# Sliding-window attention in a four-mixer decoder trunk: mask, scale and row maximum in one operation, keys ahead of the first queries left out, three reorderings

## The chip, the cores and the metric

The kernel runs on one NeuronCore of a Trainium2 chip, all four layers in one launch. The metric is the device time in microseconds, the median of several runs. A run is compared with runs of the kernel before on the same chip.

## The reference, cut to what matters

The input is a residual stream of 512 tokens by 1024 features, batch 1. Four layers follow each other; layer i adds mixer i (RG-LRU, Mamba-2 SSD, sliding-window attention, HGRN2) and then a gated feed-forward block with a short convolution. All is float32. The change is in the third mixer:

```python
q = _partial_rope(_rmsnorm(q, q_norm), cos, sin)       # 16 heads of 64
k = _partial_rope(_rmsnorm(k, k_norm), cos, sin)       # 4 heads, each shared by 4 query heads
...
scores = jnp.einsum('bnqhgd,bnkhd->bnhgqk', qb, kw) * (hd ** -0.5)
...
mask = (diff >= 0) & (diff < WINDOW) & (kpos[:, None, :] >= 0)
scores = jnp.where(mask[None, :, None, None], scores, -jnp.inf)
...
m = jnp.maximum(jnp.max(scores, axis=-1, keepdims=True), sink)
p = jnp.exp(scores - m)
denom = jnp.sum(p, axis=-1, keepdims=True) + jnp.exp(sink - m)
o = jnp.einsum('bnhgqk,bnkhd->bnqhgd', p / denom, vw).reshape(bsz, s, nq)
return o.astype(h.dtype) @ w_out
```

Queries come in four blocks of 128; a block sees its own 128 keys and the 128 before them, within a window of 128. The first block has no keys before it. The sink is one number per head, which enters the maximum and the denominator only.

## The kernel before, in words

Features lie on the partitions and the 512 tokens along the free dimension. Each weight matrix comes in panels of 128 x 1024 (8 tiles of 128 x 128) through a ring of four slots. SyncE loads panel n once GpSimd has split panel n-4. ScalarE rounds it to a big part (`round_until`, L242 to L252), GpSimd subtracts that from the panel in four pieces of 256 columns and gets the bfloat16 rest (`weights_gpsimd`, L260 to L268), and TensorE multiplies both parts: eight products of the big part and eight of the rest for a tile of 512 tokens (L295 and L305 for the projections in, L337 and L341 for those out). ScalarE rounds a panel only when TensorE has used the one four places before it.

The third mixer has 12 projected tiles of 128 rows: two of keys, eight of queries, two of values. Query tile t holds two heads. The attention is cut into 16 units: unit un treats query tile t = un // 2 (so two heads, `a` = 0 and 1) and the blocks 2m and 2m+1 of queries with m = un % 2. It has four rows of work, one for each head and block, each 128 queries by 256 keys. For the first block of even units the 256 columns are blocks 0 and 1 of the keys, and the mask takes the second 128 out.

The order of everything is written out by hand in `swa_events` (L2091 to L2128), one list that every engine walks through, taking its own events. Slot 9 is v = 0. In slot v TensorE has scores(v), products pv(v-3), a step of the out projection (`early`, for one finished y tile; SWA_FILL says how many in which slot), and transposes turn(v-2). The last slots, v = 16 to 18, have no scores and two steps each. The steps of one unit:

- TensorE, scores (L2207): four products with 64 rows into PSUM banks 5 and 6. It waits until the DVE has masked the unit before (`swa_masked`), because the banks are reused.
- DVE, `score` in `swa_vector` (L2370 to L2389): four `scalar_tensor_tensor` (L2381), PSUM times a factor per query (`b.fq`, the query's normalisation) plus mask into SBUF; then the reciprocal of the sums of unit un-1 (L2364); then, after a wait for the sink column of un, one `tensor_reduce` (L2388) over all four rows of 257 columns for the negated maximum.
- ScalarE (L2302): four exponentials of 257 columns with the sum as an accumulated result. They wait for the reduction.
- GpSimd (`swa_gpsimd`, L2404 on): `sunk` (L2417) copies the sinks into column 256 of the four rows of a score buffer; there are three buffers, so it waits for the transposes of unit un-3. `weighted` (L2425) multiplies the four rows by the reciprocals. In its queue, among the panels: sinks 0 and 1 after panel 11; weighting 0 after panel 13; after panel 14 sink 2, weighting 1, sink 3, weighting 2; after panel 15 sink 4, weighting 3, sink 5, weighting 4, and so on to weighting 15.
- TensorE, transposes (L2224): eight of 128 x 128 into banks 7 and 4, each pair after its row is weighted and after the copies of the unit before. ScalarE copies them to SBUF (L2310, two of 512 columns, `copied`, which stands behind the exponentials of unit un+1 in its queue).
- TensorE, products with the values (L2242): eight of 128 columns; then, after each odd unit, ScalarE and the DVE split the finished y tile (L2316, L2395).

After unit 15 TensorE has the first seven steps of output tile 2 and then the rest of the out projection (`out_tensor`), which needs no attention unit but the last y tile.

Of the kernel before, what the change touches and what calls it, by code (L numbers as in the profile page):

```python
# [28 lines left out]
P = 128  # L29
# [59 lines left out]
PARAMS = {}  # L89
# [1991 lines left out]
SWA_V = 10  # L2081
SWA_FIRST = 9
# [8 lines left out]
def swa_events():  # L2091

    ev, fill = [], 0
    for slot in range(SWA_FIRST + 19):
# [18 lines left out]
        if 3 <= v:  # L2113
            ev.append(("pv", v - 3, 0))
        if v >= 0:
            for _ in range(SWA_FILL[v]):
                ev.append(("early", fill // 2, fill % 2))
                fill += 1
# [27 lines left out]
def swa_tensor(pe, k):  # L2146
# [48 lines left out]
    def score(un, _):  # L2195
        t, m = un // 2, un % 2
        pe.wait_ge(k.s("swa_rotated"), 3 * rope_index(2 + t) + 3)
        if un:
            pe.wait_ge(k.s("swa_masked"), 4 * un)
        else:  # L2200
            pe.wait_ge(k.s("swa_rotated"), 3 * rope_index(1) + 3)
        for blk in range(2):
            for a in range(2):
                rows = slice(64 * a, 64 * a + 64)
                n = 2 * m + blk
                key = max(n - 1, 0) * P
                mm = pe.matmul(k.ps[:, 5 + a, blk * 256:(blk + 1) * 256], b.q[rows, t, n * P:(n + 1) * P],  # L2207
                               b.kt[rows, t // 4, key:key + 256], start=True, stop=True)
        mm.then_inc(k.s("swa_scored"), 1)

    def turn(un, _):
# [7 lines left out]
        for a in range(2):  # L2219
            for blk in range(2):  # L2220
                pe.wait_ge(k.s("swa_weighted"), 4 * un + 2 * a + blk + 1)
                for kh in range(2):
# [4 lines left out]
    def pv(un, _):  # L2227
# [7 lines left out]
        for blk in range(2):  # L2235
            n = 2 * m + blk
            for kh in range(2):
                chunk = max(n - 1, 0) + kh
                at = (2 * blk + kh) * P
                for a in range(2):  # L2240
# [3 lines left out]
                                   start=kh == 0, stop=kh == 1)  # L2244
# [14 lines left out]
def swa_scalar(act, k):  # L2259
# [36 lines left out]
    def score(un, _):  # L2296
        m, s = un % 2, b.scores[un % 3]
        act.wait_ge(k.s("swa_max"), un + 1)
        for a in range(2):
            for blk in range(2):  # L2300
                row, n = s[:, a, blk, 0:257], 2 * a + blk
                act.activation(row, row, ACT.Exp, bias=b.neg[:, m, n:n + 1], accum_out=b.sum[:, m, n:n + 1]  # L2302
                               ).then_inc(k.s("swa_exp"), 1)

    def copied(un, _):
        if un >= 2:
            act.wait_ge(k.s("swa_pv"), un - 1)
        for a in range(2):
            act.wait_ge(k.s(f"swa_turned{a}"), un + 1)
            act.activation(b.pt[:, un % 2, a, :], k.ps[:, (7, 4)[a], :], ACT.Copy).then_inc(k.s(f"swa_pt{a}"), 1)  # L2310
# [14 lines left out]
def swa_vector(dve, k):  # L2325
# [44 lines left out]
    def score(un, _):  # L2370
# [17 lines left out]
        dve.tensor_reduce(b.neg[:, m].rearrange("p (a b) -> p a b", a=2), s[:, :, :, 0:257], AX.X, ALU.max,  # L2388
                          negate=True).then_inc(k.s("swa_max"), 1)  # L2389
# [13 lines left out]

def swa_gpsimd(pool, k, panel):  # L2404
    b = SwaBuffers(k)

    def sunk(un):
        t, s = un // 2, b.scores[un % 3]
        at = PARAMS["swa_sinks"][0] + 8 * (t // 4) + t % 4
# [294 lines left out]
```

## Time and profile before

| | |
|---|---|
| median of 3 runs | 1797.73 us |
| lowest and highest | 1797.21 and 1797.99 us |
| the profiled execution, its own time | 1797.72 us |
| its span in the profile | 1795.5 us |
| TensorE busy | 1754.2 us, 98% |
| DVE, ScalarE, GpSimd busy | 65%, 63%, 68% |
| share of TensorE in the chain that ended last | 75% |

The page of a profile gives the busy time of each engine, the span in 40 slices, the chain of work that ended last and the costliest groups of instructions. PE is TensorE, DVE VectorE, ACT ScalarE, POOL GpSimd. Times inside the profile count from the start of the span. Matmuls are pipelined and their ends are modelled, so a matmul's duration is longer than its share of TensorE's time; the distance from one start to the next tells more. The same holds on the other engines: an instruction's record can overlap the next one's. The attention units lie between about 976 and 1050 us, in slices 22 and 23 of 40.

### The profile page before, as it was taken

Reading aid. Unit: us, or ns where it says so; the run is one execution under the profiler, and the core shown is the slowest. Engines: PE = TensorE matmul, PEld = TensorE weight load, DVE = VectorE, ACT = ScalarE, POOL = GpSimd, SP = SyncE. Lnnn points to the kernel's source line nnn. Section 1 sums busy time; section 2 is a strip of 40 time slices with the busy share of each in tenths; the row PEclk is TensorE's granted clock in tenths of the full one; section 3 lists DMA queues with packets and bytes.
Section 4 is the critical chain, followed back from the end, with each engine's and each line's share of the span. In section 5 each row is a group of like instructions: output and inputs, shape, how many; then the busy total and the mean of one; then the engine's idle time right before and its main releaser. Section 6 shows DMA issues by size and latency. Waiting matters only on the chain.

```text
span 1795.5 us, 25084 instructions
## 1 busy us (share of the span) xinstructions
PE 1754.2 (98%) x8752; PEld 1086.2 (60%) x8752; DVE 1166.7 (65%) x1884; ACT 1130.1 (63%) x1582; POOL 1220.6 (68%) x1776
## 2 busy tenths in 40 slices
PE   7989999999999999999999999999999999999999
PEld 4546666655565556666666666666667766566665
DVE  6886777138988855777237857774267777577720
ACT  8887666456887667666464877665444444866641
POOL 7847777876545467777875658777864444577785
PEclk9999999999999999999999999999999999999999
DMA  7333444444222235444442024444432232244443
GB/s 267 105 95 129 151 143 144 160 149 130 87 90 83 95 94 176 141 151 145 153 138 94 25 71 146 148 146 147 158 118 83 71 95 71 95 158 146 144 157 122
DMA packets 64636, 225.38 MB, mean 126 GB/s; under 512 B 7808, under 2 KB 8192, under 8 KB 64128
## 3 DMA queue, kind: packets, MB, share of 16 engines
q1 hardware_dynamic: 63936, 221.79, 37.5%
q10 hardware_dynamic: 576, 2.01, 0.3%
q8 instruction: 70, 1.15, 0.3%
q14 instruction: 54, 0.44, 0.1%
HBM read 221.57 MB, written 2.10 MB: 125 GB/s over the span
## 4 chain that ended last, share of the span: by engine, by line
PE 75%; DVE 12%; ACT 6%; issue 5%; POOL 1%; DMA 1%; SPq 0%; DVEq 0%; ACTq 0%; POOLq 0%
PE psum L295 22%; PE psum L305 21%; PE psum L337 12%; PE psum L341 12%; PE psum L1807 2%; DVE psum L1593 1%; PE psum L2207 1%; ACT w_big L250 1%; ACT psum L1462 1%; PE psum L2242 1%; DVE arena L1990 1%; DVE psum L1678 1%; DVE arena L1581 1%; DVE arena L1640 1%; DVE arena L1988 1%
## 5 line engine op out<-in xcount | busy, mean ns | idle before, releaser
L266 POOL TENSOR_TENSOR w_rest<-w_panel,w_big 128x256 bf16<-128x256 f32 x1660 | 1169.4, 742 | 526.1 <-ACT w_big L250 526.1
L295 PE MATMUL psum<-x_big,w_big 128*128 128x512 f32 x2248 | 658.1, 426 | 9.3 <-ACT x_big L387 6.9
L305 PE MATMUL psum<-x_rest,w_rest 128*128 128x512 bf16 x2248 | 555.9, 382 | 1.7 <-DVE x_rest L483 1.7
L250 ACT ACTIVATE w_big<-w_panel 128x1024 fp32r<-128x1024 f32 (+1 forms) x415 | 418.2, 1032 | 172.7 <-PE psum L341 99.5
L295 PEld LDWEIGHTS psum<-x_big,w_big 128*128 128x128 f32 x2248 | 418.3, 189 | 132.5 <-issue 25.4
L305 PEld LDWEIGHTS psum<-x_rest,w_rest 128*128 128x128 bf16 x2248 | 188.6, 98 | 283.1 <-issue 102.2
L701 DVE SCALAR_TENSOR_TENSOR psum<-ffn_raw,params,psum 128x512 f32<-128x512 f32 x352 | 264.5, 751 | 7.2 <-ACT psum L655 1.0
L693 DVE TENSOR_TENSOR ffn_raw<-psum,rstd 128x512 f32<-128x512 f32 x176 | 121.3, 691 | 139.0 <-PE psum L305 121.3
L655 ACT ACTIVATE psum<-ffn_raw,params 128x512 f32<-128x512 f32 x176 | 137.4, 782 | 101.7 <-DVE ffn_raw L693 101.3
L337 PE MATMUL psum<-g_big,w_big 128*128 128x512 f32 x704 | 199.3, 423 | 0.0
L547 DVE SCALAR_TENSOR_TENSOR x_resid<-psum,x_resid 128x512 f32<-128x512 f32 x64 | 43.8, 688 | 224.7 <-PE psum L341 216.6
L341 PE MATMUL psum<-g_rest,w_rest 128*128 128x512 bf16 x704 | 170.0, 381 | 0.0
L337 PEld LDWEIGHTS psum<-g_big,w_big 128*128 128x128 f32 x704 | 133.0, 189 | 36.2
L662 ACT ACTIVATE g_big<-psum 128x512 fp32r<-128x512 f32 x88 | 52.6, 597 | 111.3 <-DVE psum L710 111.3
L341 PEld LDWEIGHTS psum<-g_rest,w_rest 128*128 128x128 bf16 x704 | 61.1, 98 | 87.9 <-issue 26.5
L337 PE MATMUL psum<-y_big,w_big 128*128 128x512 f32 x320 | 107.8, 459 | 2.1 <-DVE y_rest L2029 1.1
L483 DVE SCALAR_TENSOR_TENSOR x_rest<-x_big,psum 128x512 bf16<-128x512 f32 x64 | 43.9, 686 | 91.5 <-ACT psum L391 91.5
L341 PE MATMUL psum<-y_rest,w_rest 128*128 128x512 bf16 x320 | 90.1, 383 | 1.8 <-POOL w_rest L266 1.8
L337 PEld LDWEIGHTS psum<-y_big,w_big 128*128 128x128 f32 x320 | 60.3, 191 | 18.5 <-issue 4.5
L710 DVE TENSOR_TENSOR psum<-psum,ffn_silu_out 128x512 f32<-128x512 f32 x88 | 61.5, 699 | 7.0 <-ACT ffn_silu_out L678 4.1
L387 ACT ACTIVATE x_big<-x_resid,shifted_gain 128x512 fp32r<-128x512 f32 x64 | 45.5, 710 | 32.1 <-DVE x_resid L547 31.6
L714 DVE SCALAR_TENSOR_TENSOR g_rest<-g_big,psum 128x512 bf16<-128x512 f32 x88 | 59.8, 680 | 2.7 <-ACT g_big L662 2.7
(263 smaller groups left out, 1814.5 us busy)
## 6 DMA issues: line engine op xcount, KB each, us to landing
w_panel<-in_up SPq DMA_DIRECT2D x176, 512.0 KB, 3.2
w_panel<-in_dn SPq DMA_DIRECT2D x64, 448.0 KB, 3.1
w_panel<-in_ssd_in SPq DMA_DIRECT2D x41, 512.0 KB, 3.6
w_panel<-in_dn SPq DMA_DIRECT2D x32, 512.0 KB, 3.2
w_panel<-in_hgrn_in SPq DMA_DIRECT2D x32, 512.0 KB, 3.6
w_panel<-in_lru_in SPq DMA_DIRECT2D x18, 512.0 KB, 3.3
w_panel<-in_ssd_out SPq DMA_DIRECT2D x16, 512.0 KB, 3.5
w_panel<-in_swa_in SPq DMA_DIRECT2D x12, 512.0 KB, 3.6
```

The source lines that it names most:

```text
L250: act.activation(k.w1[:, slot, 0:words], k.w[:, slot, 0:words], ACT.Copy, scale=(SHIFT - 1) / SHIFT).then_inc(k.s("panel_big"), 1)
L266: rest = pool.tensor_tensor(k.w2[:, slot, a], k.w[:, slot, a], k.w1[:, slot, a].bitcast(F32), ALU.subtract)
L295: pe.matmul(out, k.w1[:, slot, q * m:(q + 1) * m], k.x1[:, q, :], start=q == 0, stop=False)
L305: mm = pe.matmul(out, k.w2[:, slot, q * m:(q + 1) * m], k.x2[:, q, :], start=False, stop=q == DT - 1)
L337: pe.matmul(out, k.w1[:, slot, (q - p0) * P:(q - p0 + 1) * P], y1[:, q, :], start=q == 0, stop=False)
L341: mm = pe.matmul(out, k.w2[:, slot, (q - p0) * P:(q - p0 + 1) * P], y2[:, q, :], start=False, stop=q == kt - 1)
L655: act.activation(out, k.ffn_raw[:, j % 2, half, 2:], ACT.Identity, bias=k.p("ffn_conv_b", j + (l * 2 * FF_T + half * FF_T)), scale=k.p("ff ...
L662: act.activation(k.g1[:, j, :], k.ps[:, lin_bank(j), :], ACT.Copy, scale=1 / SHIFT).then_inc(k.s("ffn_hi"), 1)
L693: dve.tensor_tensor(k.ffn_raw[:, j % 2, half, 2:], k.ps[:, k.bank(job, i), :], k.rstd[:, :], ALU.mult).then_inc(k.s("banks_free"), 1)
L701: dve.scalar_tensor_tensor(out, k.ffn_raw[:, j % 2, half, tap:tap + S], k.p("ffn_conv_w", j + ((l * 3 + tap) * 2 * FF_T + half * FF_T)), o ...
L710: dve.tensor_tensor(out, out, k.ffn_silu[:, j % 2, :], ALU.mult).then_inc(k.s("ffn_gated"), 1)
L714: dve.scalar_tensor_tensor(k.g2[:, j, :], k.g1[:, j, :].bitcast(F32), 1 - SHIFT, k.ps[:, lin_bank(j), :], ALU.mult, ALU.add).then_inc(k.s( ...
```

## The change

It does the following.

1. One operation per row on the DVE, `tensor_tensor_reduce`, takes the scores from PSUM, adds the mask, multiplies by the query's factor, writes the row, and writes the minimum of the row and a starting value beside it. Mask, queries and sinks have their sign turned for this: the masks hold +1e30, the queries' cosine and permutation tables are negated in the setup, the sink column holds minus the sink, and the exponential has a scale of -1. The minimum is then the negated maximum. The separate reduction is gone. The starting value is the sink column, so the wait for the sink of unit un now stands ahead of the four operations. The reciprocal of unit un-1 still stands behind them.
2. The exponentials wait for their own row's result. TensorE's next scores wait for the four operations.
3. The first block of even units leaves out the second 128 keys: in the scores, the DVE's operation, the exponential, the weighting, the transposes, the copy and the products.
4. In the slots v = 16 to 18 the two steps of the out projection stand ahead of the products.
5. GpSimd: sink 4 stands ahead of panel 15, and weighting 3 and sink 5 stand between the two halves of panel 15. After it: weighting 4, sink 6, weighting 5, sink 7, and so on.

The diff, cut to its core:

```diff
-def weights_gpsimd(pool, k, n):
+def weights_gpsimd(pool, k, n, between=None):
     for at in range(0, words, PIECE):
+        if between is not None and at >= words // 2:
+            between()
+            between = None
         a = slice(at, min(at + PIECE, words))
         rest = pool.tensor_tensor(k.w2[:, slot, a], k.w[:, slot, a], k.w1[:, slot, a].bitcast(F32), ALU.subtract)
     rest.then_inc(k.s("panel_split"), 1)
...
+def swa_keys(m, blk):
+
+    return P if m == 0 and blk == 0 else 0
...
+        products = [("pv", v - 3, 0)] if 3 <= v else []
+        steps = [("early", (fill + i) // 2, (fill + i) % 2) for i in range(SWA_FILL[v])] if v >= 0 else []
+        fill += len(steps)
+        ev += steps + products if v >= 16 else products + steps
...
         if un:
-            pe.wait_ge(k.s("swa_masked"), 4 * un)
+            pe.wait_ge(k.s("swa_max"), 4 * un)
...
         for blk in range(2):
             for a in range(2):
                 rows = slice(64 * a, 64 * a + 64)
-                n = 2 * m + blk
-                key = max(n - 1, 0) * P
-                mm = pe.matmul(k.ps[:, 5 + a, blk * 256:(blk + 1) * 256], b.q[rows, t, n * P:(n + 1) * P],
-                               b.kt[rows, t // 4, key:key + 256], start=True, stop=True)
+                n, skip = 2 * m + blk, swa_keys(m, blk)
+                key, count = max(n - 1, 0) * P, 256 - skip
+                mm = pe.matmul(k.ps[:, 5 + a, blk * 256 + skip:(blk + 1) * 256], b.q[rows, t, n * P:(n + 1) * P],
+                               b.kt[rows, t // 4, key:key + count], start=True, stop=True)
         mm.then_inc(k.s("swa_scored"), 1)
...
-                row, n = s[:, a, blk, 0:257], 2 * a + blk
-                act.activation(row, row, ACT.Exp, bias=b.neg[:, m, n:n + 1], accum_out=b.sum[:, m, n:n + 1]
-                               ).then_inc(k.s("swa_exp"), 1)
+        for blk in range(2):
+            for a in range(2):
+                row, n = s[:, a, blk, swa_keys(m, blk):257], 2 * blk + a
+                act.wait_ge(k.s("swa_max"), 4 * un + n + 1)
+                act.activation(row, row, ACT.Exp, bias=b.neg[:, m, n:n + 1], scale=-1.0,
+                               accum_out=b.sum[:, m, n:n + 1]).then_inc(k.s("swa_exp"), 1)
...
     dve.wait_ge(k.s("mixer_landed"), 64)
-    for cos, perm, g in ((b.cos_k, b.perm_k, k.p("swa_k_norm")), (b.cos_q, b.perm_q, k.p("swa_q_norm"))):
-        dve.tensor_scalar(cos, b.cos, g, None, ALU.mult).then_inc(k.s("swa_setup"), 1)
-        dve.tensor_scalar(perm, b.perm, g, None, ALU.mult).then_inc(k.s("swa_setup"), 1)
+    for cos, perm, g, sign in ((b.cos_k, b.perm_k, k.p("swa_k_norm"), 1.0), (b.cos_q, b.perm_q, k.p("swa_q_norm"), -1.0)):
+        dve.tensor_scalar(cos, b.cos, g, sign, ALU.mult, ALU.mult).then_inc(k.s("swa_setup"), 1)
...
         dve.wait_ge(k.s("swa_fq"), t // 4 + 1)
+        dve.wait_ge(k.s("swa_sunk"), un + 1)
         for blk in range(2):
             for a in range(2):
-                f = 8 * t + 2 * (2 * m + blk) + a
-                dve.scalar_tensor_tensor(s[:, a, blk, 0:256], k.ps[:, 5 + a, blk * 256:(blk + 1) * 256],
-                                         b.fq[:, f:f + 1], b.mask[:, 256 * (m + blk):256 * (m + blk) + 256],
-                                         ALU.mult, ALU.add).then_inc(k.s("swa_masked"), 1)
+                f, n, skip = 8 * t + 2 * (2 * m + blk) + a, 2 * blk + a, swa_keys(m, blk)
+                dve.tensor_tensor_reduce(s[:, a, blk, skip:256], k.ps[:, 5 + a, blk * 256 + skip:(blk + 1) * 256],
+                                         b.mask[:, 256 * (m + blk):256 * (m + blk + 1) - skip], b.fq[:, f:f + 1],
+                                         s[:, a, blk, 256:257], ALU.add, ALU.min, b.neg[:, m, n:n + 1]
+                                         ).then_inc(k.s("swa_max"), 1)
         if un:
             inverse(un - 1)
-        dve.wait_ge(k.s("swa_masked"), 4 * un + 4)
-        dve.wait_ge(k.s("swa_sunk"), un + 1)
-        dve.tensor_reduce(b.neg[:, m].rearrange("p (a b) -> p a b", a=2), s[:, :, :, 0:257], AX.X, ALU.max,
...
+def swa_between(pool, k, panel):
+
+    def between():
+        swa_weighted(pool, k, 3)
+        swa_sunk(pool, k, 5)
+
+    return between if panel == 15 else None
...
 def swa_gpsimd(pool, k, panel):
...
     elif panel == 14:
         for un in (1, 2):
+            swa_sunk(pool, k, un + 1)
+            swa_weighted(pool, k, un)
+        swa_sunk(pool, k, 4)
     elif panel == 15:
+        for un in range(4, 16):
+            if 4 < un < 15:
+                swa_sunk(pool, k, un + 1)
+            swa_weighted(pool, k, un)
```

`swa_sunk` and `swa_weighted` are the former inner functions `sunk` and `weighted`; the first writes the sinks times -1 with a `tensor_scalar` in place of a copy, the second starts each row behind the keys left out. In the transposes, the products and the copies the loops begin at `swa_keys(m, blk)` in the same way.

## Rows read from the trace of the kernel before

**Rows 1.** The page, busy time by engine and the clock granted in 40 slices

```profile
PE 1754.2 (98%) x8752; PEld 1086.2 (60%) x8752; DVE 1166.7 (65%) x1884; ACT 1130.1 (63%) x1582; POOL 1220.6 (68%) x1776
...
PEclk9999999999999999999999999999999999999999
```

**Rows 2.** Chain that ended last, 1025 to 1036 us; start us, us, what

```profile
1025.44 1.06 PE psum L2207 x8
1026.50 1.02 PE psum L2242 x16
1027.53 0.43 PE psum L337
...
1029.06 1.06 PE psum L2207 x8
...
1034.77 1.02 PE psum L2224 x8
```

**Rows 3.** Waits, 970 to 1050 us; us in total, times, longest

```profile
POOL arena L2425 <- DVE arena L2364: 27.9, 15, 5.9
...
PE psum L2242 <- ACT arena L2310: 3.4, 4, 0.9
```

**Rows 4.** Timeline of TensorE after the last products; start us, us, what

```profile
1048.97 0.50 PE L337 MATMUL psum<-y_big,w_big 128*128 128x512 f32 x1
...
1049.81 1.97 PE L337 MATMUL psum<-y_big,w_big 128*128 128x512 f32 x7
```

**Rows 5.** Timeline of the DVE; the last bracket is the idle time before

```profile
931.63 1.29 DVE L2336 TENSOR_TENSOR arena<-psum,rstd 128x512 f32<-128x512 f32 x2 [1.77 <-ACT rstd L556]
...
999.95 1.22 DVE L2388 TENSOR_REDUCE arena<-arena 128x4 f32<-128x1028 f32 x1 [1.50 <-POOL arena L2417]
...
1033.85 1.66 DVE L2381 SCALAR_TENSOR_TENSOR arena<-psum,arena 128x256 f32<-128x256 f32 x4 [0.70 <-PE psum L2207]
1035.42 0.17 DVE L2364 RECIPROCAL arena<-arena 128x4 f32<-128x4 f32 x1
1035.54 1.22 DVE L2388 TENSOR_REDUCE arena<-arena 128x4 f32<-128x1028 f32 x1
```

**Rows 6.** Timeline of GpSimd

```profile
988.34 2.81 POOL L266 TENSOR_TENSOR w_rest<-w_panel,w_big 128x256 bf16<-128x256 f32 x4
991.07 0.21 POOL L2417 COPY arena<-params 128x4 f32<-128x4 f32 x1
...
999.65 0.20 POOL L2417 COPY arena<-params 128x4 f32<-128x4 f32 x1
...
1035.69 1.85 POOL L2425 TENSOR_SCALAR arena<-arena 128x256 f32<-128x256 f32 x4 [1.64 <-DVE arena L2364]
1037.48 0.19 POOL L2417 COPY arena<-params 128x4 f32<-128x4 f32 x1
```

**Rows 7.** Groups by line and form, DVE and GpSimd; count, busy us, mean ns

```profile
L701 DVE SCALAR_TENSOR_TENSOR psum<-ffn_raw,params,psum 128x512 f32<-128x512 f32 x352 | 264.5, 751 | 7.2 <-ACT psum L655 1.0
L693 DVE TENSOR_TENSOR ffn_raw<-psum,rstd 128x512 f32<-128x512 f32 x176 | 121.3, 691 | 139.0 <-PE psum L305 121.3 <-issue 17.7
...
L2381 DVE SCALAR_TENSOR_TENSOR arena<-psum,arena 128x256 f32<-128x256 f32 x64 | 26.5, 476 | 4.1 <-PE psum L2207 3.6
...
L2388 DVE TENSOR_REDUCE arena<-arena 128x4 f32<-128x1028 f32 x16 | 19.5, 1218 | 1.5 <-POOL arena L2417 1.5
...
L1040 DVE TENSOR_TENSOR_SCAN psum<-arena,psum 128x512 f32<-128x512 f32 x10 | 12.1, 1217 | 0.0
...
L2013 DVE COPY arena<-psum 128x128 f32<-128x128 f32 x8 | 2.2, 278 | 2.0 <-PE psum L1841 2.0
...
L2425 POOL TENSOR_SCALAR arena<-arena 128x256 f32<-128x256 f32 x64 | 29.6, 482 | 27.9 <-DVE arena L2364 27.9
```

**Rows 8.** Timeline of ScalarE, an accumulator read and the exponential behind it

```profile
1002.62 0.19 ACT L2302 ACTIVATION_READ_ACCUMULATOR arena<-arena 128x1 f32 x1
1002.71 0.50 ACT L2302 ACTIVATE arena<-arena 128x257 f32<-128x257 f32 x1
```

More of the change, by code:

```diff
@@ L2221, in turn @@
                 pe.wait_ge(k.s("swa_weighted"), 4 * un + 2 * a + blk + 1)
-                for kh in range(2):
+                for kh in range(swa_keys(un % 2, blk) // P, 2):
                     at = (2 * blk + kh) * P
@@ L2236, in pv @@
             n = 2 * m + blk
-            for kh in range(2):
-                chunk = max(n - 1, 0) + kh
+            k0 = swa_keys(m, blk) // P
+            for kh in range(k0, 2):
+                chunk = max(n - 1, 0) + kh - k0
                 at = (2 * blk + kh) * P
@@ L2243, in pv @@
                                    b.vt[:, chunk, 64 * head:64 * head + 64], b.pt[:, m, a, at:at + P],
-                                   start=kh == 0, stop=kh == 1)
+                                   start=kh == k0, stop=kh == 1)
         mm.then_inc(k.s("swa_pv"), 1)
@@ L2401, in swa_vector, with swa_sunk @@
             do[what](i, o)
-def swa_gpsimd(pool, k, panel):
[L2405 to L2409, printed above, removed]
-        sinks = k.par[:, at:at + 5:4].unsqueeze(2).unsqueeze(3).to_broadcast([P, 2, 2, 1])
-        if un >= 3:
-            pool.wait_ge(k.s("swa_turned1"), un - 2)
-        elif un == 2:
-            pool.wait_ge(k.s("swa_rotated"), 3 * SWA_V)
-        else:
-            pool.wait_ge(k.s("banks_free"), k.evicted("swa_in", 0))
-        pool.tensor_copy(s[:, :, :, 256:257], sinks).then_inc(k.s("swa_sunk"), 1)
-    def weighted(un):
-        m, s = un % 2, b.scores[un % 3]
-        pool.wait_ge(k.s("swa_inv"), un + 1)
-        for a in range(2):
-            for blk in range(2):
-                row, n = s[:, a, blk, 0:256], 2 * a + blk
-                pool.tensor_scalar(row, row, b.inv[:, m, n:n + 1], 1.0, ALU.mult, ALU.mult
-                                   ).then_inc(k.s("swa_weighted"), 1)
+def swa_sunk(pool, k, un):
+    b = SwaBuffers(k)
+    t, s = un // 2, b.scores[un % 3]
+    at = PARAMS["swa_sinks"][0] + 8 * (t // 4) + t % 4
+    sinks = k.par[:, at:at + 5:4].unsqueeze(2).unsqueeze(3).to_broadcast([P, 2, 2, 1])
+    if un >= 3:
+        pool.wait_ge(k.s("swa_turned1"), un - 2)
+    elif un == 2:
+        pool.wait_ge(k.s("swa_rotated"), 3 * SWA_V)
+    else:
+        pool.wait_ge(k.s("banks_free"), k.evicted("swa_in", 0))
+    pool.tensor_scalar(s[:, :, :, 256:257], sinks, -1.0, None, ALU.mult).then_inc(k.s("swa_sunk"), 1)
@@ new lines, in swa_weighted @@
+def swa_weighted(pool, k, un):
+    b = SwaBuffers(k)
+    m, s = un % 2, b.scores[un % 3]
+    pool.wait_ge(k.s("swa_inv"), un + 1)
+    for a in range(2):
+        for blk in range(2):
+            row, n = s[:, a, blk, swa_keys(m, blk):256], 2 * blk + a
+            pool.tensor_scalar(row, row, b.inv[:, m, n:n + 1], 1.0, ALU.mult, ALU.mult
+                               ).then_inc(k.s("swa_weighted"), 1)
+def swa_between(pool, k, panel):
[3 more added lines that the diff above has]
+    return between if panel == 15 else None
@@ L2493, in _ @@
             for n in range(FIRST, len(PANELS)):
[L2494 removed]
+                weights_gpsimd(pool, k, n, swa_between(pool, k, n - k.panel0["swa_in"]))
                 if raw_tile(5) <= n < raw_tile(5) + DT:
@@ L2611, in swa_table @@
     later = (key > i[:, None]) & (key <= i[:, None] + P)
-    masks = [np.where(ok, 0.0, -1e30) for ok in (key <= i[:, None], later, later)]
+    masks = [np.where(ok, 0.0, 1e30) for ok in (key <= i[:, None], later, later)]
     freq = (np.float32(ROPE_THETA) ** (-np.arange(0, ROT, 2, dtype=np.float32) / np.float32(ROT))).astype(np.float32)
```

27 lines of the change are left out of this document (6 added, 21 removed).

## The prediction

> **What bounds it now.** I read the page first, then the waits between 970 and 1050 us, the chain there, and the instructions of each engine in order. TensorE is busy for 98% of the span at a granted clock of full speed throughout, which is its 2.4 GHz level [rows 1], so only what shortens or lengthens TensorE's stretch with the 16 attention units counts. In the middle of it one unit takes 1029.06 - 1025.44 = 3.62 us on the chain, all TensorE: scores 1.06, products 1.02, and 1029.06 - 1027.53 = 1.53 for one step of the out projection and the transposes [rows 2]. Nothing else is on the chain there. TensorE does lose time at two places: at units 4 to 6, where the DVE's reduction waited 1.50 us for a sink column that GpSimd wrote only after a panel [rows 5, 6], and in the last units, where it waits for ScalarE's copies, four times, 3.4 us in all, at most 0.9 [rows 3]. The same view has the row that I put most on: GpSimd waits for the reciprocal before each unit's weighting, 27.9 us in 15 waits [rows 3]. The last products end and seven free steps begin at 1049.81 [rows 4]; from there on nothing of the change is left, and TensorE has work without a gap. So I forecast where that moment moves.
>
> **The loop that the change closes.** Before, the DVE masks unit n without asking for its sink column; only the reduction asks, and the reciprocal of unit n-1 stands ahead of that reduction. In the changed queue the order is: wait for sink n, four fused operations of n, reciprocal n-1. On GpSimd it is, as before: weighting of n-1 (it waits for that reciprocal), then sink n+1. So fused(n), reciprocal(n-1), weighting(n-1), sink(n+1), fused(n+1) follow each other strictly, and all of them are one step of the pipeline. Behind the waiting DVE stand the reciprocal and TensorE's next scores, which need the fused operations to have emptied the banks.
>
> The terms of a step. Reciprocal to weighting: 1035.69 - 1035.42 = 0.27 [rows 5, 6]. Weighting to sink: 1037.48 - 1035.69 = 1.79 [rows 6]. Sink to DVE: 999.95 - 999.65 = 0.30 [rows 5, 6]. In even units half of the rows lose 128 keys: GpSimd's operation took 482 ns for 256 columns [rows 7] and its copy 0.19 for 4 [rows 6], so 1.15 ns a column, 0.147 for 128, two rows a unit: 1.50 instead of 1.79. On the DVE, operations from PSUM took 691 ns for 512 and 278 for 128 columns [rows 7], 1.07 ns a column: 0.13 us less for each of two short rows.
>
> The fused operation is not in this trace. Call its pitch, start to start at 256 columns, c. From below: the mask that it replaces does the same two arithmetic steps on the same operands and has a pitch of (1035.42 - 1033.85)/4 = 0.39 [rows 5]; I see no reason for less. What it has more is a result on the side and a second scalar read from memory. ScalarE shows what its side result costs: the read after each exponential holds the engine from 1002.62 to 1002.71, 0.09 [rows 8]. A scalar from memory makes the 512-column operation 751 ns instead of 691 [rows 7], so 0.06 at most for a second. That gives 0.48 to 0.54, and I take 0.51. From above: the scan, which also carries a value from element to element, took 1217 ns where the plain operations take 691 [rows 7], 1.03 ns a column more; 0.39 + 0.26 + 0.09 and a share for the other scalar and for draining is 0.85.
>
> A step with n odd is then 4 x 0.51 + 0.27 + 1.50 + 0.30 = 4.11, with n even 4 x 0.51 - 0.26 + 0.27 + 1.79 + 0.30 = 4.14, against 3.62 before. TensorE alone would need less than before: two of four score products halved is 0.27, two of eight of the products 0.25, two of eight transposes about 0.25 in each even unit, so 3.62 and 2.85. It would wait over 0.8 us in a step on average.
>
> **The sum.** The loop starts with fused(2): sink 2 came at 991.07, behind the weighting of unit 0 and panel 14 [rows 6]. That weighting now starts 0.20 later (four operations of 2.04 in place of 1.57, less the 0.27 by which the scores of unit 0 are shorter, so that unit 1 comes earlier) and is 0.29 shorter, so sink 2 comes at 990.98 and fused(2) at 991.28. The two halves of panel 15 are 1.4 us each (2.81 for the four pieces of panel 14 [rows 6]) and lie beside the fused operations of units 4 and 5, whose 1.78 to 2.04 plus the hop GpSimd must wait for anyway; they cost nothing. Splitting and moving them takes away the 1.50 us wait, but that wait was once [rows 5], and the loop is in each step. Steps for n = 2 to 13, six of each kind: 49.5, so fused(14) starts at 1040.78. It ends 1.78 + 0.08 later (the last mask ended 1035.51 - 1035.42 = 0.09 behind its pitch [rows 5]), and 0.14 is taken for the way to TensorE, so the scores of unit 15 begin at 1042.78. From there TensorE has scores 1.06, products of 12 0.77, transposes of 13 1.02 [rows 2], two steps 0.97 (0.84 where no transposes follow [rows 4]), products of 13 1.02, transposes 0.77, steps 0.97, products 0.77, transposes 1.02, steps 0.97, products of 15 1.02: 10.36. Within it TensorE waits about 0.7 for GpSimd's rows of unit 14, whose reciprocal follows fused(15). That is 1053.9, against 1049.81: **4.1 us later**. The new order of the last units does what it says: a pair of steps of 0.97 fills each of three waits of up to 0.9 for the copies [rows 3], and this is in the sum.
>
> Going through all units with these rows' durations, each instruction starting when its engine and what it waits for allow, lands 0.1 us from the trace for the kernel before, and at 4.3 for the changed one. In c it is close to a line: 60 us per us of pitch (the fused operations of units 1 to 15, four each, all lie on the path). Zero is at c = 0.44.
>
> **What costs nothing.** The sign in the four setup operations adds none and they end over 1.7 us before the DVE's next work, which waited for ScalarE [rows 5]. The exponentials now start after their own row's minimum; ScalarE's four take half a microsecond each [rows 8] in a step of 4.1, so this hides. The DVE loses 1.2 us of reduction per unit [rows 7] and gains 4 x 0.12, but it waits in that time. No DMA is added or moved; panel 16 on depends on TensorE's use of panel 12, and shifts with it.
>
> **Two rules beside the rows.** The mask's pitch of 0.39 at 256 columns [rows 5] is more than two plain operations of 512 columns let expect: those have a pitch of 1.29 - 0.69 = 0.60 [rows 5, 7], less 256 columns of 1.07 ns 0.33. The difference is what a scalar from memory costs. The Trainium skill (Vector Engine (DVE) Microarchitecture Reference, Measured stream behaviour on trn2) gives 1.0417 ns a column and about 75 ns an instruction, also for programs of several micro-operations: an estimate of 0.34 for the new operation, by which the change would gain some 6 us. The mask's row is slower than this rule already without a side result, so I go by the row.
>
> ScalarE's rows show an activation with a sum as two records, the second of which takes its own 0.09 [rows 8]; for the DVE no row has such a pair. The Trainium skill (VectorE: DVE Perf Modes, Two Vector instructions with no wait between them) says that it is so there too: "an op that also writes out its accumulator is two instructions". That is against the change.
>
> **Rivals.** (1) It ends on the other side, not slower: the pitch is that of the mask or below 0.44, the loop's step is then 3.6 to 3.8, hardly longer than before, and the gains at units 4 to 6, in the skipped keys and in the last units prevail. At 0.39 the line gives -3.1 (1794.6 us), at the 0.33 of an operation to which the scalar costs nothing -6.7 (1791.0). It decides below 0.44. For it: the same operands. Against: the side result. 0.22. (2) The read of the side result waits until the main operation has drained: 0.475 + 0.12 = 0.60 (the mask's duration [rows 7] and the distance of the small reciprocal), +9.5, 1807.2 us. ScalarE's read does not wait so [rows 8]. 0.20. (3) Half rate, as in the scan: 0.85, +24.5, 1822.2 us. The reduction runs 1028 columns in 1218 ns [rows 7], full rate, which speaks against. 0.06. The forecast's own case, 0.44 to 0.56, has 0.52.
>
> **Numbers.** The profiled execution took 1797.72 us, the median of the runs is 1797.73, so the sum is carried over as it is: 1797.7 + 4.1 = 1801.8. The range goes from the mask's pitch, 1794.6, to a little past rival 2, 1808.5. About 0.2%, 3.6 us, is what a measurement can tell from no change; slower by that needs c over 0.50, faster needs c under 0.38. Half of the forecast's case is over 0.50: 0.26 + 0.20 + 0.06 is 0.52 slower. Faster has 0.11, half of rival 1, and 0.37 is left for the same.
>
> **What would show it.** Right: GpSimd's sink of unit n+1 ends just before the first fused operation of n+1 in every unit, the DVE's idle time before them is put down to GpSimd's sinks, steps of about 4.1 us alternate little, TensorE waits 0.7 to 1.3 us before each scores, and no longer for copies in the last units. Wrong: a chain that is all TensorE with steps of 3.6 and 2.9, or DVE idle before the fused operation ended by TensorE's scores. The pitch decides the size.

## The result and the profile after

| | median | against before |
|---|---|---|
| before, 12 runs | 1797.72 us | |
| changed, 12 runs | 1801.88 us (1801.05 to 1802.4) | 1.0022, interval 1.0014 to 1.0030, or 4.2 us more |

The page of the changed kernel answers to [rows 1] and to the table of before. TensorE's share falls from 98% to 97%, and on the chain from 75% to 71%:

```profile
PE 1742.6 (97%) x8543; PEld 1083.0 (60%) x8704; DVE 1149.9 (64%) x1932; ACT 1127.2 (63%) x1582; POOL 1218.2 (68%) x1776
...
PE 71%; DVE 14%; issue 5%; ACT 5%; POOL 3%; another core or an unknown queue 1%; DMA 1%; SPq 0%; DVEq 0%; ACTq 0%; POOLq 0%
```

The waits between 970 and 1055 us (us in total, times, longest) answer to [rows 3]. POOL L2433 is the weighting, L2374 the reciprocal, L2392 the fused operation, L2423 the sink column, L2215 the scores:

```profile
POOL arena L2433 <- DVE arena L2374: 35.1, 16, 6.0
DVE arena L2392 <- POOL arena L2423: 28.1, 14, 2.7
...
PE psum L2215 <- DVE arena L2392: 12.3, 12, 2.7
```

GpSimd's wait for the reciprocal grew from 27.9 us in 15 waits to 35.1 in 16, and the second row did not exist before: 14 times the fused operations waited for a sink column, 28.1 us in all. TensorE's wait for ScalarE's copies (3.4 us in [rows 3]) is gone; in its place TensorE waits before the scores, twelve times, for the fused operations: 2.71 us once, and 0.59 to 1.38 the other times, where 0.7 to 1.3 was forecast.

The chain in the middle of the units (start us, us, what) answers to [rows 2], where it was all TensorE:

```profile
1018.19 1.84 POOL arena L2433 x4
1020.03 0.20 POOL arena L2423
...
1020.39 0.49 DVE arena L2392
...
1022.34 0.10 DVE arena L2374
...
1022.52 1.62 POOL arena L2433 x4
1024.15 0.20 POOL arena L2423
...
1024.52 0.63 DVE arena L2392 x3
```

One round can be read off: weighting of an odd unit from 1018.19, sink, fused operations from 1020.39, reciprocal, weighting of an even unit from 1022.52, sink, fused operations from 1024.52. TensorE does not occur.

The DVE's timeline (start us, us, what, idle time before) answers to [rows 5]:

```profile
991.72 0.41 DVE L2392 CUSTOM_DVE_ANT_0 arena<-psum,arena 128x128 f32<-128x128 f32 x1 [2.68 <-POOL arena L2423]
...
1020.39 0.54 DVE L2392 CUSTOM_DVE_ANT_0 arena<-psum,arena 128x256 f32<-128x256 f32 x1 [1.72 <-POOL arena L2423]
1020.86 0.08 DVE L2392 DVE_READ_ACCUMULATOR2_ANT arena<- 128x1 f32 x1
1020.86 0.54 DVE L2392 CUSTOM_DVE_ANT_0 arena<-psum,arena 128x256 f32<-128x256 f32 x1
...
1022.26 0.17 DVE L2374 RECIPROCAL arena<-arena 128x4 f32<-128x4 f32 x1
1024.52 0.41 DVE L2392 CUSTOM_DVE_ANT_0 arena<-psum,arena 128x128 f32<-128x128 f32 x1 [2.09 <-POOL arena L2423]
1024.85 0.08 DVE L2392 DVE_READ_ACCUMULATOR2_ANT arena<- 128x1 f32 x1
...
1041.25 0.41 DVE L2392 CUSTOM_DVE_ANT_0 arena<-psum,arena 128x128 f32<-128x128 f32 x1 [2.08 <-POOL arena L2423]
```

The new operation is recorded as two instructions, the custom operation and an accumulator read. From one to the next it is 1020.86 - 1020.39 = 0.47 us at 256 columns and 1024.85 - 1024.52 = 0.33 at 128. The four of a unit, up to the reciprocal behind them, take 1022.26 - 1020.39 = 1.87 us here and 1.86 in other odd units, so the pitch is 0.466. The read is recorded at the same start as the next operation.

GpSimd's timeline answers to [rows 6]. The half panel at 999.71 is the first of the two halves of panel 15; behind it GpSimd still waits 0.67 us for the reciprocal:

```profile
999.71 1.41 POOL L269 TENSOR_TENSOR w_rest<-w_panel,w_big 128x256 bf16<-128x256 f32 x2
1001.79 1.84 POOL L2433 TENSOR_SCALAR arena<-arena 128x256 f32<-128x256 f32 x4 [0.67 <-DVE arena L2374]
...
1022.52 1.62 POOL L2433 TENSOR_SCALAR arena<-arena 128x128 f32<-128x128 f32 x4 [2.31 <-DVE arena L2374]
1024.12 0.23 POOL L2423 TENSOR_SCALAR arena<-params 128x4 f32<-128x4 f32 x1
```

TensorE's timeline, from the first scores to the seven free steps that stood at 1049.81 in [rows 4]:

```profile
977.01 0.93 PE L2215 MATMUL psum<-arena 64*128 64x128 f32 x8
...
993.55 1.52 PE L2215 MATMUL psum<-arena 64*128 64x256 f32 x8 [2.71 <-DVE arena L2392]
...
1054.34 1.89 PE L340 MATMUL psum<-y_big,w_big 128*128 128x512 f32 x7
```

From the first scores to those seven steps it is 1054.34 - 977.01 = 77.33 us, against 1049.81 - 976.63 = 73.18 in the kernel before, whose first scores began at 976.63. I call this the attention stretch below: 4.15 us of the 4.16 lie in it. In some runs of the kernels below, and of the kernel before beside them, about 6 us more went lost ahead of the third mixer, for a reason that is not known (in the profile of `two_steps_kept` the first scores begin at 983.08 instead of 977); the attention stretch is free of that.

### The profile page after: what moved, and what is told of

It reads as the page before. It is cut to its first block, busy times and chain, and to the rows that moved or that the text cites. A ratio compares the mean times of both kernels' runs of the same rounds, so it can differ in the third digit from the quotient of the medians.

```text
span 1800.1 us, 24873 instructions
## 1 busy us (share of the span) xinstructions
PE 1742.6 (97%) x8543; PEld 1083.0 (60%) x8704; DVE 1149.9 (64%) x1932; ACT 1127.2 (63%) x1582; POOL 1218.2 (68%) x1776
## 4 chain that ended last, share of the span: by engine, by line
PE 71%; DVE 14%; issue 5%; ACT 5%; POOL 3%; another core or an unknown queue 1%; DMA 1%; SPq 0%; DVEq 0%; ACTq 0%; POOLq 0%
PE psum L298 21%; PE psum L308 20%; PE psum L340 12%; PE psum L344 11%; PE psum L1810 2%; POOL arena L2433 1%; DVE psum L1596 1%; DVE arena L2392 1%; POOL w_rest L269 1%; ACT w_big L250 1%; ACT psum L1465 1%; DVE arena L1993 1%; DVE psum L1681 1%; DVE arena L1584 1%; DVE arena L1643 1%
## 5 line engine op out<-in xcount | busy, mean ns | idle before, releaser
L308 PE MATMUL psum<-x_rest,w_rest 128*128 128x512 bf16 x2137 | 538.7, 382 | 8.0 <-DVE x_rest L486 1.7
L344 PE MATMUL psum<-g_rest,w_rest 128*128 128x512 bf16 x677 | 165.4, 381 | 1.2
L344 PE MATMUL psum<-y_rest,w_rest 128*128 128x512 bf16 x298 | 83.7, 383 | 2.5 <-POOL w_rest L269 1.8
```

The costliest lines, as they stand in the source:

```text
L308: mm = pe.matmul(out, k.w2[:, slot, q * m:(q + 1) * m], k.x2[:, q, :], start=False, stop=q == DT - 1)
L344: mm = pe.matmul(out, k.w2[:, slot, (q - p0) * P:(q - p0 + 1) * P], y2[:, q, :], start=False, stop=q == kt - 1)
```

## The experiments

The loop theory is the prediction's: the wait for the sink column, now ahead of the fused operations, closes a circle through the queues of the DVE and GpSimd, and its length is the pace. Its rival, called the price theory, puts the loss down to the new operation and its accumulator read themselves. All kernels are compared with runs of the kernel before on the same chip. A distance to the changed kernel or to `start_apart` is a plain difference of medians, some of them from different chips, on which the kernel before took 1797.72 to 1798.16 us; so some 0.4 us of it can be the chip. The attention stretch of the profiled run is given beside the median.

| kernel | median us | its before | difference | stretch us |
|---|---|---|---|---|
| changed | 1801.88 | 1797.72 | +4.2 | 77.3 |
| before_wait_ahead | 1805.8 | 1798.05 | +7.8 | 82.4 |
| inverse_first | 1799.86 | 1798.05 | +1.8 | 74.9 |
| sink_ahead | 1793.09 | 1798.05 | -5.0 | 68.2 |
| start_apart | 1789.83 | 1798.05 | -8.2 | 65.3 |
| slower_pitch | 1808.29 | 1798.16 | +10.1 | 80.9 |
| start_apart_slower_pitch | 1791.14 | 1798.16 | -7.0 | 66.4 |
| two_steps_kept | 1789.93 | 1798.16 | -8.2 | 65.2 |
| keys_kept | 1806.11 | 1798.16 | +8.0 | 81.4 |
| order_alone | 1795.76 | 1797.94 | -2.2 | 71.3 |
| gpsimd_order_before | 1805.02 | 1797.94 | +7.1 | 80.2 |
| start_apart_old_end | 1791.93 | 1797.94 | -6.0 | 67.1 |
| start_apart_copy_shared | 1790.23 | 1797.94 | -7.7 | 65.6 |

### The circle put into the kernel before

```diff
         dve.wait_ge(k.s("swa_fq"), t // 4 + 1)
+        dve.wait_ge(k.s("swa_sunk"), un + 1)
         for blk in range(2):
...
         dve.wait_ge(k.s("swa_masked"), 4 * un + 4)
-        dve.wait_ge(k.s("swa_sunk"), un + 1)
         dve.tensor_reduce(
```

> The kernel before with one line moved: the wait for the sink column of unit n stands ahead of the four masks, not ahead of the reduction. Loop theory (mask, reciprocal n-1, weighting n-1, sink n+1, mask n+1 in a strict circle): a step becomes 4 x 0.39 + 0.27 + 1.79 + 0.30 = 3.93 us instead of 3.62, and the exponentials come later; walked through unit by unit 8.2 us slower than the kernel before. Price theory (what costs is the new DVE operation and its accumulator read, the wait's place is of no account): within 1 us of the kernel before.

Measured: 7.8 us slower, ratio 1.0044 (1.0030 to 1.0058); the profiled run, 1807.44 us, was its longest. The DVE's timeline, and GpSimd's under it:

```profile
1019.47 1.66 DVE L2382 SCALAR_TENSOR_TENSOR arena<-psum,arena 128x256 f32<-128x256 f32 x4 [1.03 <-POOL arena L2417]
1021.04 0.17 DVE L2364 RECIPROCAL arena<-arena 128x4 f32<-128x4 f32 x1
...
1023.42 1.66 DVE L2382 SCALAR_TENSOR_TENSOR arena<-psum,arena 128x256 f32<-128x256 f32 x4 [0.43 <-POOL arena L2417]
```

```profile
1021.31 1.84 POOL L2425 TENSOR_SCALAR arena<-arena 128x256 f32<-128x256 f32 x4 [1.97 <-DVE arena L2364]
1023.09 0.19 POOL L2417 COPY arena<-params 128x4 f32<-128x4 f32 x1
```

A step is 1023.42 - 1019.47 = 3.95 us (3.93 expected). No instruction was added or replaced: the place of one wait makes the kernel slower than the whole change did, and it is of account, against the price theory. What the new operation costs beside it is left to the kernels below.

Two steps are longer than 3.95. Here panel 15 stands whole between weighting 2 and sink 4, so the circle carries it once: from the masks of unit 3 to those of unit 4 it is 6.69 us. And from unit 5 to unit 6 it is 5.07, because the masks waited for scores that came late; TensorE ran at a granted clock of 0.50 from 1004 to 1010 us, after a gap of 3.51 us:

```profile
1004.33 2.08 PE L2207 MATMUL psum<-arena 64*128 64x256 f32 x8 [3.51 <-DVE arena L2382]
...
1011.58 1.66 DVE L2382 SCALAR_TENSOR_TENSOR arena<-psum,arena 128x256 f32<-128x256 f32 x4 [2.15 <-PE psum L2207]
```

So about 1.1 us of what this kernel loses is the lower clock's, which the circle brought with it through TensorE's gap, and not the circle's length.

### The circle cut at three places

```diff
# inverse_first, on the changed kernel
+        if un:
+            inverse(un - 1)
         dve.wait_ge(k.s("swa_sunk"), un + 1)
         for blk in range(2):
...
-        if un:
-            inverse(un - 1)
# sink_ahead
-            if 4 < un < 15:
-                swa_sunk(pool, k, un + 1)
+            if un + 2 < 16:
+                swa_sunk(pool, k, un + 2)
             swa_weighted(pool, k, un)
# start_apart
+    dve.tensor_scalar(b.start, k.par[:, sinks0:sinks0 + 16], -1.0, None, ALU.mult).then_inc(k.s("swa_setup"), 1)
...
-        dve.wait_ge(k.s("swa_sunk"), un + 1)
+        dve.wait_ge(k.s("swa_setup"), 5)
...
-                                         s[:, a, blk, 256:257], ALU.add, ALU.min, b.neg[:, m, n:n + 1]
+                                         b.start[:, at + 4 * a:at + 4 * a + 1], ALU.add, ALU.min, b.neg[:, m, n:n + 1]
...
+        act.wait_ge(k.s("swa_sunk"), un + 1)
```

In `sink_ahead` the sinks 4 and 5 also stand ahead of the weightings of 2 and 3.

> The changed kernel with the reciprocal of unit n-1 moved ahead of the wait for sink n and of the fused operations of n. Loop theory: the circle is cut at this place, but the DVE now stands until the exponentials of n-1 are done and starts the fused operations of n only then; walked through, 3.4 us faster than the changed kernel, about 0.3 us over the kernel before. Price theory: nothing of the price is removed and the DVE waits more, so equal to the changed kernel or slower.

Measured: 2.0 us under the changed kernel, 1.8 over before (1.0014, 1.0005 to 1.0022). The sign is that of the loop theory. Of the 3.4 us that it expected, 2.0 came in the medians and 2.45 in the stretch. The DVE now stands for ScalarE's exponentials:

```profile
DVE arena L2374 <- ACT arena L2311: 19.5, 10, 2.9
```

> The changed kernel with GpSimd's order turned in each unit: sink n+2 stands ahead of the weighting of n, not behind it; every instruction is the same. Loop theory: the fused operations of n+2 no longer wait for the weighting of n; walked through, 9.8 us faster than the changed kernel and 6 us faster than the kernel before, the DVE waits for scores or for the transposes of n-1. Price theory: no change against the changed kernel, within 1 us.

Measured: 8.8 us under the changed kernel and 5.0 under before (0.9973, 0.9962 to 0.9983). It has the same instructions as the changed kernel; only GpSimd's order differs. By the loop theory it was to be 9.8 and 6. The waits moved to where the theory has them, to the transposes and the scores:

```profile
POOL arena L2423 <- PE psum L2232: 13.3, 10, 1.5
...
DVE arena L2392 <- PE psum L2215: 9.8, 11, 1.5
```

> The changed kernel, but the fused operation takes its starting value from a table of the 16 negated sinks made once in the setup, and only the exponentials wait for the sink column. GpSimd's order is untouched. Loop theory: the circle is cut, 12.9 us faster than the changed kernel and 9.2 us faster than the kernel before, TensorE without gaps and in steps of 3.6 and 2.9 us. Price theory: within 1 us of the changed kernel; the fused operations and accumulator reads are all still there, with one more small operation in the setup.

Measured: 12.0 us under the changed kernel and 8.2 under before (0.9955, 0.9942 to 0.9967). It beats both kernels of the case; only `two_steps_kept` and `start_apart_copy_shared`, below, come within 0.4 us of it. Its chain from 1015 to 1022 us:

```profile
1015.60 1.09 PE psum L2252 x16
...
1017.35 0.66 PE psum L2233 x6
1018.01 1.06 PE psum L2216 x8
1019.07 0.81 PE psum L2252 x12
1019.88 0.43 PE psum L340
...
1022.30 1.09 PE psum L2252 x16
```

All TensorE again; from one unit's products in 16 matmuls (1015.60) to the next such (1022.30) a pair of units takes 6.70 us, against 7.24 in the kernel before and 8.19 in the changed one (1028.58 - 1020.39). By the expected steps of 3.6 and 2.9 it would have been 6.5, which is part of why the gain is 0.9 to 1.0 us smaller than expected. The fused operations start when the scores or the transposes end, not behind a sink:

```profile
1012.52 0.54 DVE L2397 CUSTOM_DVE_ANT_0 arena<-psum,arena 128x256 f32<-128x256 f32 x1 [0.60 <-PE psum L2216]
...
1015.71 0.41 DVE L2397 CUSTOM_DVE_ANT_0 arena<-psum,arena 128x128 f32<-128x128 f32 x1 [1.15 <-PE psum L2233]
```

### The pitch of the fused operation, with and without the circle

```diff
+                dve.wait_ge(k.s("swa_spare"), 4 * un + n + 1)
+                dve.reciprocal(b.spare[:, 0:4], b.spare[:, 4:8]).then_inc(k.s("swa_spare"), 1)
```

> The changed kernel with one small DVE operation (a reciprocal of 4 columns on a spare tile) behind each fused operation, 64 in all, and one memset in the setup. It raises the pitch by 0.09 to 0.12 us, a reciprocal's own distance in the traces. Loop theory: each of them lies on the path, 60 us for each us of pitch, so 5.4 to 7.2 us slower than the changed kernel. Theory that TensorE or ScalarE sets the pace and the DVE's waits are idle time without cost: no change.

The first fused operation of a unit now takes 0.57 us to the next (1013.41 to 1013.98), the others 0.53, where it was 0.466. Over the four, up to the reciprocal of the former unit (L2377), it is 1015.56 - 1013.41 = 2.15 us in place of 1.87, so 0.07 for each and not the 0.09 to 0.12 expected:

```profile
1013.41 0.54 DVE L2395 CUSTOM_DVE_ANT_0 arena<-psum,arena 128x256 f32<-128x256 f32 x1 [1.74 <-POOL arena L2428]
...
1013.88 0.17 DVE L2400 RECIPROCAL arena<-arena 128x4 f32<-128x4 f32 x1
1013.98 0.51 DVE L2395 CUSTOM_DVE_ANT_0 arena<-psum,arena 128x256 f32<-128x256 f32 x1
...
1014.50 0.51 DVE L2395 CUSTOM_DVE_ANT_0 arena<-psum,arena 128x256 f32<-128x256 f32 x1
...
1015.56 0.14 DVE L2377 RECIPROCAL arena<-arena 128x4 f32<-128x4 f32 x1
```

Three runs took 1805.4 to 1806.1 us, the profiled one among them with 1805.38, and three 1810.5 to 1811.3. The median, 6.4 us over the changed kernel, lies between and says little; the size is read from the stretch, which is 3.55 us longer than in the changed kernel, or 3.55/0.07 = 51 us per us of pitch. The steps are about 4.33 and 4.40 us in place of 4.06 and 4.13.

> The same 64 small DVE operations in the kernel whose fused operations start from a table. The circle is cut there, so the DVE has slack: walked through, 2.0 to 3.7 us slower than that kernel (two thirds of it where the DVE comes close to TensorE's 2.9 us steps), less than half of what the same operations cost with the circle. If the pitch cost the same 60 us per us here, the circle would not be what makes it costly.

Measured: 1.3 us over `start_apart` in the medians, 1.1 in the stretch. The same operations cost under a third of the 3.55 us that they cost with the circle, and less than was expected.

### The fused operation itself

```diff
-        dve.wait_ge(k.s("swa_sunk"), un + 1)
...
-                dve.tensor_tensor_reduce(...)
+                dve.scalar_tensor_tensor(s[:, a, blk, skip:256], k.ps[:, 5 + a, blk * 256 + skip:(blk + 1) * 256],
+                                         b.fq[:, f:f + 1], b.mask[:, 256 * (m + blk):256 * (m + blk + 1) - skip],
+                                         ALU.mult, ALU.add).then_inc(k.s("swa_masked"), 1)
         if un:
             inverse(un - 1)
+        dve.wait_ge(k.s("swa_sunk"), un + 1)
+        for blk in range(2):
+            dve.wait_ge(k.s("swa_masked"), 4 * un + 2 * blk + 2)
+            dve.tensor_reduce(b.neg[:, m, 2 * blk:2 * blk + 2], s[:, :, blk, swa_keys(m, blk):257], AX.X, ALU.min
+                              ).then_inc(k.s("swa_max"), 1)
```

> The changed kernel with its parts 3, 4 and 5 (keys left out, last units, GpSimd's order) and its signs, but masks by the former operation and two separate minimum reductions per unit, one for each block, ahead of which alone the wait for the sink stands. Loop theory: no circle, walked through 8.7 us faster than the kernel before, 12.9 faster than the changed one. Price theory: the fused operations cost 4 us more than what they replace at most, so 1 to 4 us faster than the changed kernel.

In this kernel TensorE's scores wait for the masks, and the exponentials for the reduction of their block; these two lines are left out above.

Measured: 8.2 us under before (0.9955, 0.9938 to 0.9971), the same as `start_apart`. So the other parts of the change are worth 8.2 us, and the fused operation with its wait takes 12 us away from them; freed of the wait it is worth nothing here and costs nothing either. With this the price theory falls. Its DVE is busier, but within the time that TensorE gives it:

```profile
1018.25 1.66 DVE L2391 SCALAR_TENSOR_TENSOR arena<-psum,arena 128x256 f32<-128x256 f32 x4
...
1019.91 1.25 DVE L2399 TENSOR_REDUCE arena<-arena 128x2 f32<-128x514 f32 x2
```

### Keys, GpSimd's order, last units

```diff
# keys_kept, on the changed kernel
-    return P if m == 0 and blk == 0 else 0
+    return 0
# gpsimd_order_before, on the changed kernel
-        swa_sunk(pool, k, 4)
...
-        for un in range(4, 16):
-            if 4 < un < 15:
+        for un in range(3, 16):
+            if un < 15:
                 swa_sunk(pool, k, un + 1)
...
-    return between if panel == 15 else None
+    return None
# order_alone, on the kernel before
-        if 3 <= v:
-            ev.append(("pv", v - 3, 0))
...
+        ev += steps + products if v >= 16 else products + steps
# start_apart_old_end
-        ev += steps + products if v >= 16 else products + steps
+        ev += products + steps
```

> The changed kernel without part 3: all units treat all 256 columns. The keys left out shorten TensorE, which waits in every step, and also the fused operations (0.27 us in even units) and GpSimd's weighting (0.21 in even units), which are on the circle. Loop theory: seven even steps on the DVE and six on GpSimd, 3 us and a little for the last units, walked through 4.0 us slower than the changed kernel. Theory that only TensorE's work counts: 0.75 us in each of eight even units, 6 us.

Measured: 4.2 us over the changed kernel in the medians, 4.1 in the stretch. The keys left out pay even with the circle, through the DVE's and GpSimd's shorter work and not through TensorE's, as the loop theory has it: the steps are 4.35 us, but for the one named below, where they were 4.06 and 4.13. The 6 us of the other theory were not reached.

> The changed kernel without part 5: sink 4 behind panel 15, then weighting 3 and so on, no halves. The circle now carries the whole panel 15 once (four pieces, 2.8 us) between the weighting of 2 and sink 4, of which part was idle time. Loop theory: 2.8 us slower than the changed kernel, and only there; the steps after unit 5 are the same 4.1 us. If part 5 only fills idle time, no change.

Measured: 3.1 us over the changed kernel, 2.9 in the stretch. The step from unit 3 to unit 4 is 6.87 us instead of 4.13, and the others are as in the changed kernel. GpSimd's order was thus worth its 2.8 us; without it the circle would have cost more.

> The kernel before with part 4 alone: in the last three slots the two steps of the out projection stand ahead of the products. Theory: three waits of 0.9 us for the copies are filled, but the last transposes then wait for GpSimd's rows and ScalarE's exponentials instead; walked through, 1.8 us faster than the kernel before. If the order only moves the wait and the chain through ScalarE sets the end, under 0.5 us.

Measured: 2.2 us under before (0.9987, 0.9978 to 0.9996), 1.9 in the stretch.

> The kernel with the starting values in a table, without part 4. Walked through, 1.7 us slower than with it: the waits for the copies in the last units are back, as in the kernel before. If part 4 was of use only because the circle had made the last units late, no change.

Measured: 2.1 us over `start_apart`, 1.9 in the stretch. The order of the last units is worth about 2 us with or without the rest.

> The kernel with the starting values in a table, and the second of ScalarE's two copies per unit (the probabilities of the second head) moved to the DVE, behind the fused operations and the reciprocal in its queue. ScalarE is on that kernel's chain in units 10 to 13. If ScalarE's load is what is left (3.1 us of 3.35 per unit), 1 to 2 us faster than that kernel; if TensorE is, no change within 0.5 us; the DVE's slack of 0.6 to 1.2 us per unit must hold the copy of 0.6. Walked through unit by unit: no change.

```diff
+    def copied(un, _):
+        if un >= 2:
+            dve.wait_ge(k.s("swa_pv"), un - 1)
+        dve.wait_ge(k.s("swa_turned1"), un + 1)
+        skip = swa_keys(un % 2, 0)
+        dve.tensor_copy(b.pt[:, un % 2, 1, skip:], k.ps[:, 4, skip:]).then_inc(k.s("swa_pt1"), 1)
```

Measured: 1790.23 against 1789.83 us, the stretch 65.6 against 65.3: no change. ScalarE's place on the chain of `start_apart` was not worth anything: with its copy moved, TensorE's lines make up 84% of the chain from 1000 to 1040 us, and the time is the same.

## Why the prediction was right

**The circle.** It is there as named, with the same links in the same order, and a chain of DVE and GpSimd alone. Shown by three kernels that cut it and gained 2.0, 8.8 and 12.0 us, and by one that has it without any other edit and lost 7.8, of which about 1.1 is the lower clock.

**The terms of a step.** They were each off, and the errors cancelled. The pitch is 0.466 and not 0.51, which takes 0.18 off a step. The short rows are 0.13 shorter on the DVE, as taken. GpSimd's weighting of even units lasts 1.60 and not 1.50 (1022.52 to 1024.12), since its operation on 128 columns takes 371 ns where 335 was worked out: from 256 to 128 columns the time falls by 111 ns, and not by the 147 of a line drawn through a copy of 4 columns. From sink to fused operation it is 1024.52 - 1024.12 = 0.40 and not 0.30. So steps are 4.06 (even, 1028.58 - 1024.52) and 4.13 (odd, 1024.52 - 1020.39) where 4.14 and 4.11 stood.

One step, from 1028.58 to 1033.06, took 4.48. The sink had ended at 1032.54, and no wait in the trace accounts for the other 0.35 us. It is not the chance of one run: the same step, from unit 11 to unit 12, is 0.35 too long in `keys_kept`, `gpsimd_order_before` and `sink_ahead`, and it is not in `slower_pitch`. Its cause stays open.

Over twelve steps, from 991.72 to 1041.25, it is 49.5 us, as in the prediction. That it agrees to a tenth is luck: without the long step it would be 49.2.

**The start of the circle.** Fused(2) came at 991.72, 0.44 after the forecast, but the whole mixer began 0.38 later in this profile.

**The last units.** From fused(14) to the seven steps it is 1054.34 - 1041.25 = 13.1, and 1053.9 - 1040.8 = 13.1 in the prediction. The waits for the copies are gone. The circle goes on through fused(15) and weighting 14, and only then does the chain pass to TensorE for good, in the middle of the transposes of unit 14:

```profile
1047.45 1.63 POOL arena L2433 x4
...
1049.12 0.44 PE psum L2232 x2
```

TensorE's wait for these rows was taken at 0.7 us and came out at about that: its six transposes from 1047.96 took 1.60 us, where six took 0.88 at 1041.10.

**What costs nothing.** The halves of panel 15 lie beside the fused operations: GpSimd still waits 0.67 us behind the first and 0.94 behind the second. The exponentials and the setup do not occur on the chain.

**The rivals.** (1) Its range of pitches was not reached, 0.466 lies 0.03 above the 0.44 where it would have decided, but by the prediction's line that pitch alone would have given 1.5 us, which it counts as no change. The other terms made up the rest, so the point where the change breaks even lies lower than the 0.44 of the line: an estimate from the measured 4.15 us, the 0.466 and the slope of 60 is 0.40. That the outcome fell to "slower" was thus not owed to a pitch over 0.50, as the chances had it. The 0.39 of the mask and the 0.33 of a free scalar did not come. (2) and (3) fell: the read is recorded at the start of the next operation and waits for nothing, and the 1.04 ns a column, (0.466 - 0.333)/128, is no more than the 1.07 that the prediction read for plain operations.

**The rules beside the rows.** The estimate of 0.34 for the new operation, which the prediction worked out from the figures of the Trainium skill (Vector Engine (DVE) Microarchitecture Reference, Measured stream behaviour on trn2), was too low by 0.13. The page's slope of 1.0417 ns a column agrees with the 1.04 here; the fixed part is 0.20 us here (0.466 less 256 columns of 1.04 ns) and not about 0.075. That an operation which writes out its accumulator is two instructions (the Trainium skill, VectorE: DVE Perf Modes, Two Vector instructions with no wait between them) agrees with the records. Read and second scalar together cost 0.07 of pitch over the mask's 0.39; no run tells one from the other.

**The slope.** 60 us per us of pitch was forecast; the added operations gave 3.55/0.07 = 51 with the circle and 1.07/0.07 = 15 without it. The long step of 0.35 us stands in the changed kernel and not in `slower_pitch`; with it set aside the first is 3.90/0.07 = 56.

## What to carry to other kernels

When two operations are fused, every wait of the second becomes a wait of the first. Here the wait for a sink column moved from behind the masks and the reciprocal to ahead of them, and that closed a circle through two in-order queues whose length, not any engine's load, became the pace. Before such a change, write down for each wait what stands behind it in its queue and in the queue of whoever posts it; a small operand that comes late (here 4 numbers a partition) is better taken from a place that is filled once.

## What was not expected of the hardware

TensorE's granted clock was 1.00 in each slice before. In the changed kernel it fell after TensorE had stood for 2.71 us before the scores at 993.55, in the windows below (us of the window, busy time of each engine, granted clock, DMA share, GB/s), and it was back at 1.00 from 998:

```profile
990.00:994.00 4.00, 1.29 (x12) 1.09 (x12) 1.77 (x9) 3.88 (x12) 1.96 (x4) 1.00 0.38 102
994.00:996.00 2.00, 2.00 (x18) 1.35 (x16) 0.21 (x1) 0.16 (x2) 1.62 (x5) 0.54 0.14 57
996.00:998.00 2.00, 2.00 (x14) 1.52 (x10) 1.83 (x9) 0.37 (x1) 0.07 (x1) 0.60 0.00 0
998.00:1002.00 4.00, 3.02 (x33) 2.29 (x34) 2.08 (x10) 4.00 (x14) 3.33 (x8) 1.00 0.00 0
```

From 995 to 997 it was 0.50 of full speed, the lower of its two levels, 1.2 GHz. The scores at 993.55 took 1.52 us in place of 1.13. It cost nothing here, since the chain ran through the DVE and GpSimd: the steps from 991.72 and 995.79 are 4.07 and 4.13, like the later ones. In `before_wait_ahead` it was 0.69 in the mean from 1000 to 1010 us, and there it cost a step 1.1 us.

The gap alone does not tell whether the clock falls. `sink_ahead` has the same gap at the same place, and its clock stayed at 1.00:

```profile
993.45 1.14 PE L2215 MATMUL psum<-arena 64*128 64x256 f32 x8 [2.71 <-DVE arena L2392]
```

```profile
994.00:996.00 2.00, 2.00 (x24) 1.50 (x21) 0.31 (x1) 0.06 (x1) 1.52 (x4) 1.00 0.09 37
```

`keys_kept` kept 1.00 behind a gap of 2.77 us. What decides it, no run here shows.

The first fused operation began 0.17 us after the end of the sink column that it waited for (1024.52 against 1024.12 + 0.23), where the reduction before began 0.10 after it ([rows 5, 6], 999.95 against 999.65 + 0.20). The fused operation reads that column as a scalar and not in its stream; that this is the reason was not tried, and it can't be all of it: in `before_wait_ahead` a mask that does not read the column at all began 0.14 us after it (1023.42 against 1023.09 + 0.19).
